# The first three products of each pair moved into the pair before, 64x64 products interleaved over four quarters of the array, modulation rows in four column groups

## What is computed

```
sh1, sc1, g1, sh2, sc2, g2 = silu(c) @ ada_w + ada_b            # 6 rows of 1024, for both token groups
h = rmsnorm(x) * (1 + sc1) + sh1
z = h @ w_in                                                    # in blocks of 128 columns
r, k, v, wl, al, gl = dwconv3(z[rwkv columns])
kk = k * k_k;  kk = kk / max(sqrt(sum(kk*kk)), 1e-12)
g = sigmoid(gl) @ g_up;  w, a = f(tanh(wl) @ w_up), sigmoid(al @ a_up)     # for 2 directions
out_a = groupnorm(wkv7_scan(r, w, k, v, -kk, kk*a)) , plus a bonus, times g
out_b = neighbourhood attention (8 heads),  out_c = retention (8 heads) * silu(gate)
x = x + g1 * rmsnorm((gates * (out_a, out_b, out_c) summed) @ w_out)
x = x + g2 * rmsnorm(conv_ffn(rmsnorm(x) * (1 + sc2) + sh2))
```

## Time and profile before

| what | us |
|---|---|
| median of 3 runs (lowest, highest) | 2028.66 (2023.75, 2029.55) |
| the profiled execution, its own time | 2028.39 |
| its span, first to last instruction | 2026.2 |
| TensorE busy | 1890.5 (93%) |
| VectorE / ScalarE / GpSimd busy | 1005.3 / 939.4 / 942.6 |
| mean granted TensorE clock | 0.979 of full |

### The profile page before, as it was taken

How to read it: one execution, slowest core, us unless ns; L and a number is a source line. 1 busy time by engine, 2 the same in 40 slices (tenths; PEclk the granted TensorE clock), 3 DMA queues, 4 the chain that set the end, 5 groups by cost and what they waited for, 6 DMA issues and landing times.

```text
span 2026.2 us, 41588 instructions
## 1 busy us (share of the span) xinstructions
PE 1890.5 (93%) x17864; PEld 1707.3 (84%) x17864; DVE 1005.3 (50%) x1516; ACT 939.4 (46%) x1766; POOL 942.6 (47%) x767
## 2 busy tenths in 40 slices
PE   5899999999999889999978999999999997999997
PEld 1887878787999779999948788787879996999996
DVE  3574756475612355551156566574655133455502
ACT  4554645454533454443355455453554334544432
POOL 1434435160666536666426052433516664466663
PEclk8999999999999989999989999999999999999998
DMA  7314142332443323334353241414224332234342
GB/s 291 104 53 147 55 133 79 111 102 88 136 125 125 104 73 124 121 123 126 132 214 107 62 131 55 136 55 135 77 98 147 124 125 83 94 125 125 125 125 73
DMA packets 65414, 231.52 MB, mean 114 GB/s; under 512 B 7376, under 2 KB 11856, under 8 KB 64592
## 3 DMA queue, kind: packets, MB, share of 16 engines
q1 hardware_dynamic: 59040, 215.21, 32.7%
q10 hardware_dynamic: 6192, 13.66, 1.9%
HBM read 223.58 MB, written 5.26 MB: 113 GB/s over the span
## 4 chain that ended last, share of the span: by engine, by line
PE 78%; DVE 11%; ACT 4%; issue 3%; POOL 2%; DMA 2%; ACTq 0%; SPq 0%; DVEq 0%; POOLq 0%
PE psz L471 55%; PE psw L471 20%; DVE work L1353 3%; ACT work L947 3%; DMA ring<-in_w 2%; DVE work L1362 2%; POOL ringlo L1728 1%; DVE part L1353 1%; PE psz L479 1%; ACT whi L947 1%; PE psw L479 1%; DVE rstd L1362 1%; DVE work L1356 1%; POOL work L1764 1%; DVE work L1359 0%
## 5 line engine op out<-in xcount | busy, mean ns | idle before, releaser
L1728 POOL TENSOR_TENSOR ringlo<-ring,whi 128x512 fp32r<-128x512 f32 x608 | 809.7, 1355 | 755.6 <-ACT whi L947 755.6
L471 PE MATMUL psz<-hhi,whi 128*128 128x386 f32 x1696 | 587.2, 346 | 23.2 <-POOL ringlo L1728 14.6
L471 PE MATMUL psz<-hlo,whi 128*128 128x386 f32 x1696 | 577.5, 340 | 0.0
L471 PE MATMUL psz<-hhi,ringlo 128*128 128x386 f32 x1696 | 576.3, 340 | 0.0
L947 ACT ACTIVATE whi<-ring 128x1024 fp32r<-128x1024 f32 x304 | 320.1, 1053 | 134.1 <-PE psz L471 125.7
L471 PE MATMUL psw<-work 64*64 64x64 f32 (+4 forms) x9024 | 347.5, 231 | 17.5 <-issue 9.0
L471 PEld LDWEIGHTS psw<-work 64*64 64x64 f32 (+2 forms) x9024 | 293.4, 136 | 72.1 <-issue 54.4
L471 PEld LDWEIGHTS psz<-hhi,whi 128*128 128x128 f32 x1696 | 320.9, 189 | 36.0 <-issue 18.6
L471 PE MATMUL psz<-part,whi 128*128 128x386 f32 x1344 | 346.6, 339 | 3.8 <-DVE work L1353 1.7
L471 PEld LDWEIGHTS psz<-hlo,whi 128*128 128x128 f32 x1696 | 322.9, 190 | 2.1
L471 PEld LDWEIGHTS psz<-hhi,ringlo 128*128 128x128 f32 x1696 | 321.1, 189 | 0.0
(11 more groups left out here) (105 smaller groups left out, 1700.6 us busy)
## 6 DMA issues: line engine op xcount, KB each, us to landing
ring<-in_w SPq DMA_DIRECT2D x400, 512.0 KB, 3.5
pk<-in_pk ACTq DMA_DIRECT2D x8, 832.0 KB, 4.5
const<-in_const SPq DMA_DIRECT2D x1, 1795.0 KB, 9.9
work<-in_x SPq DMA_DIRECT2D x1, 1544.0 KB, 6.8
work<-in_x ACTq DMA_DIRECT2D x1, 1544.0 KB, 9.0
out_x<-work ACTq DMA_DIRECT2D x1, 1544.0 KB, 5.6
work<-out_x ACTq DMA_DIRECT2D x1, 1544.0 KB, 8.8
out_x<-work SPq DMA_DIRECT2D x4, 386.0 KB, 2.4
```

What stands on the lines that cost most here:

```text
L471: ins = nc.tensor.matmul(out, a, b, start=start, stop=stop, skip_group_check=True)
L1728: L.do(G.tensor_tensor(out, a, b, op), S[sig] if sig else None)
```

## The change

It does these things, in both layers:

1. Dense r, k, v of pairs 1 to 3 leave the start of their pair. Their 24 steps of three products stand in the tail of the pair before (`next_steps`), and with them go their splits, their convolution taps and the head tiles of kk (`next_tap`, `key_tiles`). The stream of blocks keeps its order. The late modulation rows are issued 16 steps earlier on average, within the levels and just behind them.
2. At a pair's start the head sums come first, nq stands ahead of the decay products and nk, and g moves behind rg and the rv transposes. On VectorE `scale_rwkv` and `scale_ret` stand inside the two directions' loop and `finish` and the bonus behind it, ahead of attention 0. On GpSimd the low part of rq moves behind kd and Lx of direction 0, that of rk behind its end values, then the bias.
3. In the levels' products, wm and u the two heads alternate inside each x, and for head 1 rows and columns of the array are crossed, so that four products in a row use the four 64x64 quarters. Head 1's matrices therefore lie in the other half of the partitions: VectorE transposes head 0 (128x384) and then head 1 in two halves across (`across`, 64x384 each), where one transpose of 128x768 stood; ScalarE's copy of art is in six pieces, where there were two. Head 1 does not start its products after head 0's any more: both wait for the same predicated copies. The g0 products and the last level's xt keep two quarters.
4. In the head, each block holds 256 columns for four column groups, the four run side by side, and the sums of squares stand in one piece (before block 6 in layer 0, before block 10 in layer 1).
5. Idle products: 8 of 128x256 behind the turned rows of the head, 11 behind the last sum of squares ahead of FFN up (`keep_warm`), whose results nobody reads.
6. `pk` is loaded in two parts, the decay matrices and g's early.

```diff
@@ head, TensorE
-                    for jp in range(2):
-                        for k in range(KT):
-                            for i in range(2):
-                                j = 2 * jp + i
-                                mm(psw[32 * j:32 * j + 2, 1, :], cs[:, k, :], ring2[b % RING][:, i, :], k == 0,
...
-                            if 0 <= i < KT:
-                                sum_squares(0, (i,))
+                    for b in range(2 * KT):
+                        if b == (10 if layer else 6):
+                            sum_squares(0)
+                        jp, k = divmod(b, KT)
+                        loaded(b)
+                        for j in range(4):
+                            mm(psw[32 * j:32 * j + 2, 1, 256 * jp:256 * jp + 256], cs[:, k, :],
...
                     mod_turned(0, modr[:, 0:512])
+                    keep_warm(8)
                     dense3(ZH, 0, hsp, ("h_lo", 0))
@@ start of a pair, TensorE
+                        def next_steps(n):
+                            if p + 1 == PAIRS:
+                                return
+                            for _ in range(n):
+                                i, k = divmod(ahead[0], KT)
+                                zi, j = zb + ZI["r"] + i, bb + 10 + i
+                                if k == 0:
+                                    opened(zi)
+                                    pe.wait_ge(*after("w_lo", 2 * j + 2))
+                                three(z(zi), j, k, hsp[k], k == 0, k == KT - 1, "z_done" if k == KT - 1 else None)
+                                ahead[0] += 1
...
+                            key_sums()
+                            dense(zb + ZI["nq"], bb + 3)
+                            pe.wait_ge(*at_of("yroot_ready", p - 1, 0))
+                            pe.wait_ge(*at_of("rroot_ready", p - 1, 0))
+                            lora_up()
+                            dense(zb + ZI["nk"], bb + 4)
+                        dense(zb + ZI["nv"], bb + 5)
+                        dense(zb + ZI["rq"], bb + 6)
...
+                        turned(zb + ZI["rvt"], zb + ZI["rv"], mixed[2][p])
+                        mm(opened(zb + ZI["g"]), pk[:, PK["g_up"]:PK["g_up"] + P], lgl, sig="z_done")
                         values_mm(0)
@@ levels, TensorE
-                            for hb in range(2):
-                                pe.wait_ge(*at_of("x_ready", p, 0 if lv == 1 else 2 * (lv - 2) + hb + 1))
-                                for x in range(6):
+                            pe.wait_ge(*at_of("x_ready", p, 0 if lv == 1 else 2 * (lv - 2) + 2))
+                            for x in range(6):
+                                for hb in range(2):
                                     for c in range(2):
-                                        mm(psw[hc(c), g_bank(lv, hb), CH * x:CH * x + CH], au[hc(c), hb, x, 0, 0:CH],
+                                        mm(psw[hc(c ^ hb), g_bank(lv, hb), CH * x:CH * x + CH], au[hc(c), hb, x, 0, 0:CH],
                                            xv[hc(c), hb, x, :], sig="gl_done" if (x, c) == (5, 1) else None)
@@ VectorE
+                    def across():
+                        for c in range(2):
+                            flip(tvv[hc(1 - c), 1:2], xv[hc(c), 1:2], "tv_ready" if c else None)
...
-                                flip(tvv, xv, "tv_ready")
+                                flip(tvv[:, 0:1], xv[:, 0:1])
+                                across()
...
+                            if p:
+                                (scale_rwkv, scale_ret)[d](p - 1)
...
+                        if p:
+                            finish(p - 1)
+                        dve.wait_ge(*after("bon_done", p + 1))
+                        tt(bonus, w(1), vc, sig="bon_used")
@@ GpSimd
-                        pool.wait_ge(*after("kk_sq", p + 1))
-                        low(sb_ + 6)
-                        pool.wait_ge(*after("pk_in", 16 * (p + 1)))
...
-                        low(sb_ + 7)
...
-                            if d:
-                                low(sb_ + 8)
+                            low(sb_ + (8 if d else 6))
...
+                            if d:
+                                continue
+                            low(sb_ + 7)
+                            pool.wait_ge(*after("pk_in", 16 * (p + 1)))
@@ ahead of FFN up, TensorE
                     sum_squares(2)
+                    keep_warm(11)
```

More of the change, by code:

```diff
@@ L57 @@
     SPLIT += range(PAIR0 + PAIR_BLOCKS * _p, PAIR0 + PAIR_BLOCKS * _p + 10)
+ZI = {name: i for i, name in enumerate(("nq", "nk", "nv", "rq", "nvt", "rk", "rv", "rg", "rvt", "g", "f0", "f1", "f2",
+                                        "f3", "f4", "f5", "ada", "r", "k", "v"))}
 SM = len(SPLIT)
@@ new lines, in _ @@
+                        if p == 0:
+                            for i in (1, 2):
+                                dense(ZP + i, bb + i)
+                            dense(zb + ZI["nq"], bb + 3)
+                            dense(zb + ZI["nk"], bb + 4)
+                            key_sums()
+                            pe.wait_ge(*after("lora_in", 2))
+                            lora_up()
+                        else:
+                            key_sums()
+                            dense(zb + ZI["nq"], bb + 3)
@@ L1073, in _, with query_in @@
-                        act.wait_ge(*at_of("kkn_done", p, 0))
-                        run(Pi, w(0), ACT.Sqrt, "kkn_root")
+                        if p == 0:
+                            for i, dst in enumerate((rc, kc_, vc)):
+                                centre_tap(dst, ZP + i, "conv", 4 * i)
+                                split(sb_ + i + 3)
+                        def query_in():
+                            seen(zb + ZI["nq"])
+                            run(nq, z(zb + ZI["nq"]), free=zb + ZI["nq"], scale=0.125)
+                            split(sb_ + 6)
@@ L1226, in _ @@
                             run(u0[:, hb], six(w(2 + hb, 0, 384)), sig="u_ready")
+                        late_rows(p, zb + ZI["ada"])
+                        split(sb_ + 11)
                         for c in range(2):
```

325 lines of the change are left out of this document (182 added, 143 removed).

## The result

| | us |
|---|---|
| changed kernel, median of 4 runs (lowest, highest) | 2110.85 (2107.5, 2112.25) |
| kernel before, median of 4 runs | 2026.2 (2023.44, 2029.55) |
| ratio, 95% interval | 1.041 (1.0396 to 1.0424) |
| profiled execution, its span | 2112.25, 2110.4 |

The account below looks back on a forecast made before the run. It took TensorE's chain (78%, VectorE 11%) as the bound. Its terms, -4.4 - 41 + 47 + 15.6 - 8.4 - 6.7 - 2.2 = 0 against the profiled 2028.39, gave 2028 us, range 2007 to 2049.

Parts of the forecast that it names:

- T to the masks' products: From a pair's head sums (T) to the masks' products, pairs 1 to 3: +6.5 waits, 1.3 clock; +47 for six.
- the second bullet of "Start, pairs 1 to 3": VectorE's chain to the first maximum ends at T+32.3, TensorE stands at attention 1 at T+28.7: wait 3.6.
- lower bound: Starts of pairs 1 to 3: no clock loss and VectorE 3 us faster, +2.5 a start.
- the second case: Waits at a pair's start are short: six starts cost 3.5 each instead of 7.8, 2002 us, halfway 2014; chance 0.34.
- The third case: The clock falls at each start of pairs 1 to 3: some +20, 2048 us; chance 0.24.
- Masks' products to the next T: Levels and tail of pairs 0 to 2: -0.55 per pair and -6.8 per transition; -44 for six.
- X: Start of the last level's xt products; the next pair's head sums were forecast at X+31.8.
- Start of pair 0: First pair of each layer: TensorE waits 5.7 for rq's low part; 7.8 with g, +15.6 for both layers.
- Quarters: Levels, wm and u: 8.6 less TensorE time per pair, mostly off the path; -0.55 per pair, -4.4 in all.
- The fourth case: Four quarters do no more than two, a bank being taken by both row halves: +46, 2074 us; chance 0.06.
- Heads: Both layers' heads: column groups, sums in one piece and idle products bring the first products earlier, -6.7.
- tail of pair 3: Each layer's last pair: no dense steps, fewer late rows, norm ends at X+22 instead of X+26.2; -8.4 for two.

Follow-up runs that it names:

- e10: Changed kernel with the low part of rq ahead of kd of direction 0 on GpSimd in all pairs; 2101.2 us, 1.0366.
- e5: Changed kernel with 18 idle products 128x256 in pairs 1 to 3 just before TensorE's wait for attention 0's maximum; 2098.8 us, 1.0370.
- e14: Kernel before with part 3 alone, and attention 3's maximum ahead of the two transposes across on VectorE; 2015.5 us, 0.9949.
- e8: Kernel before with part 3 alone (four quarters, VectorE's transposes in three pieces, art in six); 2038.5 us, 1.0049.
- e15: Changed kernel with attention 3's maximum ahead of the two transposes across, nothing else; 2084.5 us, 1.0293.
- e2: Changed kernel with GpSimd's order of before in pair 0 alone: low parts of rq and rk and the bias ahead of direction 0; 2100.2 us, 1.0368.
- e4: Changed kernel with g behind the masks' products; 2095.7 us, 1.0324.
- e13: Kernel before with parts 4 and 5, but the sums of squares one by one between the blocks as before; 2016.9 us, 0.9942.
- e1: Changed kernel with scale_ret behind attention 0's maximum, scale_rwkv behind attention 1, finish and the bonus behind attention 2 on VectorE; 2075.5 us, 1.0234.
- e16: Kernel before with part 3 (attention 3's maximum ahead of transposes across), column groups with sums apart and idle products, without parts 1 and 2; 2007.7 us, 0.9908.
- e3: Changed kernel with the first two dense steps of the tail behind mi and nn instead of ahead of them; 2111.5 us, 1.0398.
- e7: Changed kernel with five edits: late finish, pair 0's low parts early, tail's first dense steps behind nn, g late, head sums between blocks; 2035.0 us, 1.0048.

## Why the prediction was wrong

- **T to the masks' products: +78 instead of +47.** The step that failed is the second bullet of "Start, pairs 1 to 3", VectorE at T+32.3. The maximum came at T+37.3, and TensorE waited 7.8 us for it, where I had 3.6. The order of the passes was right, and so was the scan's start (334.41, T+9.5 with the sigmoid's wait of 3.0 in it); from there to the end of the maximum it takes 27.7 us, and I had 23.2:

```profile
341.96 3.24 DVE L1440 TENSOR_TENSOR work<-work 128x386 f32<-128x386 f32 x2
345.23 2.46 DVE L1631 TENSOR_TENSOR_SCAN work<-const,work 128x386 f32<-128x386 f32 x1
...
354.12 3.16 DVE L1440 TENSOR_TENSOR work<-work 128x386 f32<-128x386 f32 x2
```

  In pair 2 before, both pairs of passes took 1.02 and the scan 0.96: these three rows are 5.9 us longer, and small differences in the other passes and waits give 1.3 of it back. Each of them stands beside a GpSimd instruction:

```profile
341.58 3.20 POOL L1836 TENSOR_TENSOR ringlo<-ring,whi 128x512 fp32r<-128x512 f32 x2
344.74 2.14 POOL L1836 TENSOR_TENSOR pk<-pk,const 128x768 f32<-128x768 f32 x1
...
353.74 3.12 POOL L1836 TENSOR_TENSOR ringlo<-ring,whi 128x512 fp32r<-128x512 f32 x2
```

  I priced the moved passes (a reciprocal with its product at 3.15, finish) but not that the old ones would run beside the low parts of rq and rk and the bias, which GpSimd now has in the same 27 us. My lower bound let the chain become 3 us faster; the upper had it no slower at all. That GpSimd slows these passes the traces show. Over the whole trace of the change, the 34 such tensor_tensor passes with no tensor_tensor of GpSimd beside them take 0.55 to 0.58 each; the 52 that lie wholly beside one take 0.56 to 1.66, half of them 1.28 or more. The reciprocals take 2.53 to 2.57 in either place. And e10 is a test of one pass: there no tensor_tensor of GpSimd runs beside the second scan of pair 2 (the bias is done at 342.48, and what follows it, from 343.10 on, is the tensor_scalar of kd), and the scan takes what it took before:

```profile
342.93 0.96 DVE L1631 TENSOR_TENSOR_SCAN work<-const,work 128x386 f32<-128x386 f32 x1
```

  The chain as a whole is 0.9 us shorter in e10 (26.9), since other passes stand beside GpSimd instead (the pair ahead of this scan takes 3.76). No run took GpSimd's work away, so that all of the 4.5 us would go with it is not shown. The terms that I listed add up to T+32.1 here and to T+26.1 for rv's low part, where I wrote 32.3 and 26.5, and the lower bound of +2.5 a start does not go with the 3.5 that the second case uses; none of this decides anything.
- **The clock at a start: 3.6 us instead of 1.3** in pair 2 (sum over 358 to 370), 2.1 to 3.6 in the six. The wait is 7.8 long, not 3.6. The third case, a fall at each start, came true, with a size too small (+20): I had priced two falls of 2 us beside waits that I took as known. e5 keeps the clock up and gets 2.6 us a start back.
- **Masks' products to the next T: -10 instead of -44.** Two terms. In the levels, +1.0 instead of -0.55 (34.5 against 33.5): I counted the transposes' half microsecond, and overlooked that attention 3's maximum is queued behind them. Pair 2 is one of two pairs in which the clock stays up behind the wait that this makes; in the other six it falls and costs 1.6 to 1.7 us, and where the trace shows X their levels take 2.0 to 2.5 longer than before. e14 against e8 and e15 against the change show the place of that maximum to be worth 20 and 24 to 26 us, the largest thing that the prediction missed altogether. In the tail of pair 2, X+36.2 instead of X+31.8: 1.2 more of wait for r's low part, 1.55 for mi and nn at half clock behind it (3.88 against 2.33), and 1.6 by which my sum of the parts behind them was too short (from 424.2 to 447.5 TensorE never stops: 23.3, I had 21.7).
- **Start of pair 0: right** (+8.2 and +8.0, forecast 7.8 each), with the wait of 5.7 at its place. e2 says that taking it away gives back half, 4.2 each, because the wait for rv's low part returns.
- **g: right** in size (1.49 against 1.7), and it is more than its wait: e4 gains 15 to 17 us in eight pairs.
- **Quarters: right for TensorE.** 48 records in 0.93 with their overlap, forecast 0.76. The fourth case, a time that stays at 1.6, is out. By the rule in the Trainium skill, TensorEngine Tiling (Array Packing), Gotcha 1: PSUM Pressure, the row halves that write one bank should have taken turns. Each head has a bank of its own here, and both row halves write it, so by that rule two products could be under way at once and no more. An estimate, if the time goes by columns: 18 idle products of 256 columns take 7.93 us in e5, so 24 of 64 columns take 2.6 one at a time, and 1.3 two at a time. They take 0.86 (0.93 less the overlap), so more than two are under way, and this trace disagrees with the rule.
- **Heads: +2.5 instead of -6.7.** Layer 0 loses 2.3 where I had -2.4, layer 1 loses 0.2 where I had -4.3. The step that failed: "the sums in one piece 6.4" was costed as TensorE's time, and not as time in which the ring's slots stay taken. e13 keeps the column groups and lets the sums alone, and gains 12 us, where I had 8.9 for parts 4 and 5 together. What the idle products give apart from the column groups no run shows.
- **Behind pair 3: -2.8 instead of -11.7.** The levels took 2.4 to 2.5 us more in each layer, since level 1's wait stands in pair 3 as well and the clock falls behind it; I had -0.55. From X to the merge products layer 1 gains 3.3; layer 0 gains only 0.6, for there the clock is at 0.50 from 544 to 550, behind waits of 1.76 (no releaser) and 1.09 us. So "tail of pair 3", -8.4 for two, came to -3.9. Ahead of FFN up the gain was 0.9 and 1.5 us, 2.4 where I had 2.2: this term was right. Some 1.5 in layer 0's FFN up are left unexplained.

## What to carry to other kernels

When work moves to a stretch in which another engine is busy, price the passes that stand there already again, not only the moved ones: here the moved passes were priced right, and old ones beside GpSimd took 3.2 us where they had taken 1.0. When an instruction on a queue grows, list what stands behind it on that queue and who waits for it; here 1.2 us of transposes ahead of one maximum cost 20 us, twice what part 3 gives without them there. And read the granted clock behind each wait before and after an edit: a wait of 2.1 us cost 3.1 more in six pairs of e8 and nothing more in pair 2 of the change, and where e1 took a wait away and e5 filled it, a part of the clock's cost came back behind the next wait.

## What the runs showed of the chip

TensorE's time lost at half clock went from 24.6 to 62.5 us with the change, and down to 19.7 in e16 and 20.9 in e13. The clock falls behind single waits of 2.1 us (e8, 354.47) though not behind each of them: in the change the same wait at 387.39 left it at full speed, and what decides is open. Behind level 1's wait of 0.7 us (e14) it fell in none of the eight pairs.

A tensor_tensor pass of VectorE over 128x386 takes 0.56 us alone and up to 1.66 beside a tensor_tensor of GpSimd, a scan 0.96 and up to 2.47, a reciprocal 2.57 in either place.

The gaps that the trace puts down to "issue", 0.97 to 2.1 us in the tail before and 2.54 in e3, stand where the ring's loads come in a burst (in e7 a gap of 1.83 us from 387.6, with the DMA engines busy for 0.98 to 1.02 of the stretches from 382 to 388); what they are stays open.
